# A decoder step with 16 experts on one core: order of the down weights, bf16 token tables, expert 0's table first, tail transposes between halves

## The chip, the cores and the metric

The kernel runs on one core of a Trainium2 chip. The metric is the time of one execution on the device in microseconds. The kernel before was timed three times: 1049.95 us median, 1045.94 to 1050.38.

## The reference

One layer of a decoder trunk serves 512 prompt tokens and 8 sample tokens (520 in all, width 1024). A joint projection feeds three attention-like heads (a gated recurrence, differential attention, dilated windows); their outputs are multiplied with `w_out` and added to the input. Then comes the part that the change touches:

```
u = rmsnorm(h) * norm_ffn
group = argmax(u @ rgw + rgb)                 # 4 groups
top 2 of the group's 4 experts, gate = p(group) * softmax(their logits)
for e in 16 experts:
    y += gates[:, e] * ((silu(u @ wg[e]) * (u @ wu[e])) @ wd[e])   # 1024 -> 512 -> 1024
h = h + y
h = h + sigmoid(rmsnorm(h) * norm_ple @ pgw) * (p @ ppw)
y_out = rmsnorm(h) * norm_final
```

All arrays are float32. An expert has three weights of 2 MB: gate and up (1024 x 512) and down (512 x 1024), 100 MB for the sixteen.

## The kernel before

There are five instruction streams, one per engine, and all order is by semaphores. Up to about 630 us the kernel computes the projection, the heads and `w_out` (L2262), and for each of five token tiles the normalised rows (stored to `u2d` in DRAM by SP, L750) and the router's logits.

**Routing.** VectorE turns the logits into one-hot choices, and `C` (128 tokens x 5 tiles x 16 experts) says which experts a token uses. TensorE multiplies `C` with a strict triangle `tri` and with `ones` (L2337 to L2341, float32, into PSUM bank 1): each token's rank within its expert and the count of each expert. VectorE sorts the experts by count (`key`, `beats`, `rnk`), plans the overflow, and gives every choice a row `rk` and a table column `tk` (L1804 to L1830). `Rsel` (L1831) and `Tsel` (L1832, L1833) are one-hot matrices of those, `Tsel` scaled by the token number, and ten float32 products (L2345) make of them a table of 33 columns with the token numbers of each expert job. VectorE computes the table of steps first and only then copies the token table to `idxall` (L1845). GpSimd copies one column of it (L862) and gathers the rows from `u2d` by an indirect DMA (L865), one gather for each step. The ranks of experts 0, 1 and 2 are fixed, so they are always the first three steps.

**Expert steps.** 15 static steps and a loop (one turn here) for the overflow follow. Step s handles 32 x `STEP_JOBS[s]` token rows: 3 jobs in steps 0, 1, 2, 6, 8, 10, 12, 14, 4 jobs in step 4, 2 jobs in the others. The first two jobs are one phase, what is left a second phase. In a phase:
- `rows` (L2354) transposes the gathered rows, VectorE's `front` (L1865) scales them to `xgT`;
- `gate_up` (L2369, and L2365 in the second phase of a 3-job step) multiplies 32 rows at a time with gate and up, four 32-column blocks of the array side by side. In the second phase of a 3-job step the four blocks hold the halves of gate and up, and a half is columns j, j+1 of every four: the moving operand is read with a step of four floats;
- ScalarE applies silu, VectorE multiplies, `columns_of_h` (L2389) transposes, ScalarE copies, `down` (L2406, and L2402 in such a second phase) multiplies with the down weights, VectorE copies the result, ScalarE's queue stores it to `Yd`.

TensorE runs a phase's `gate_up` before the `down` of the phase before.

**Weights.** `SLOT` has eight places of 2 MB, used in turn by the three loads of each step. SP issues the loads in order (L732); load k of step s waits until the `gate_up` or `down` that used its slot has ended (`released`). Loads of steps 1 and 0 and two of step 2 are issued before the routing, at 572 and at 630 us; the others wait. Each load moves 128 runs of 16 KB. After the loop's loads SP issues `ple_w_gate` (L775), `ple_w_proj` (L777), the p rows (L780) and `norm_final` (L781). The queues of SP, ScalarE and GpSimd use the same 16 DMA engines.

**Tail.** From 950 us TensorE transposes the p rows (L2320) and multiplies them (L2331), and then for each of five tiles: GpSimd gathers the two expert results, VectorE combines them (L1903, L1905), ScalarE computes the norm (L1143 to L1146), VectorE scales (L1913), TensorE transposes (`columns`, L2238), VectorE copies to `hnT` (L1920), TensorE multiplies with `ple_w_gate` in two halves of 16 records (`ple`, L2485; L2248 for the sample tile), ScalarE applies the sigmoid (L1239, L1242), VectorE finishes (L1662, L1663) and applies the last norm (L1669). `columns(i + 1)` stands behind both halves of `ple(i)`.

## Time and profile before

| | us |
|---|---|
| median of three runs | 1049.95 |
| the profiled execution | 1055.73 |
| its span | 1054.0, mean granted clock 0.948 |
| TensorE busy in it | 948.5 (90%) |
| VectorE, ScalarE, GpSimd busy | 376.9, 238.2, 81.5 |
| routing, from the last logits to the first expert product | 631.4 to 663.5 |
| expert steps | 663.5 to 950.1 |
| products of the p rows, then the tiles | 950.2 to 1051.6 |

Some single instructions that the text uses: VectorE had been idle for 2.67 us before its first `w_out` addition (L1707) at 564.35; `rows` of step 0 took 1.53 us from 660.91 and `front` 0.97 from 662.47; the operations between 642.28 (L1812) and 649.40 (L1832) end with the positions of all choices; of the products of the p rows the first eight records took 5.40 us from 954.36, the next eight 3.44; tile 1's scaling (L1913) ended at 981.77; the steps 8 and 9 began at 808.51 and the next at 842.34; SP issued the load of `ple_w_gate` at 922.95.

The profile is of one execution. Busy times of TensorE are of modelled ends: a float32 product shows as two records. The chain of waits follows the end of the program back from releaser to releaser; "landing" of a DMA is the time from its issue to its completion.

### The profile page before, as it was taken

Reading aid. Unit: us, or ns where it says so; the run is one execution under the profiler, and the core shown is the slowest. Engines: PE = TensorE matmul, PEld = TensorE weight load, DVE = VectorE, ACT = ScalarE, POOL = GpSimd, SP = SyncE. Lnnn points to the kernel's source line nnn. Section 1 sums busy time; section 2 is a strip of 40 time slices with the busy share of each in tenths; the row PEclk is TensorE's granted clock in tenths of the full one; section 3 lists DMA queues with packets and bytes.
Section 4 is the critical chain, followed back from the end, with each engine's and each line's share of the span. In section 5 each row is a group of like instructions: output and inputs, shape, how many; then the busy total and the mean of one; then the engine's idle time right before and its main releaser. Section 6 shows DMA issues by size and latency. Waiting matters only on the chain.

```text
span 1054.0 us, 15610 instructions
## 1 busy us (share of the span) xinstructions
PE 948.5 (90%) x6377; PEld 492.1 (47%) x6377; DVE 376.9 (36%) x791; ACT 238.2 (23%) x600; POOL 81.5 (8%) x96
## 2 busy tenths in 40 slices
PE   3996999999999998986969983899999999998886
PEld 2453556655456785663444543333333333333442
DVE  4305644564226755355542226111111111111445
ACT  3115212221232332443221110000000000003335
POOL 1000000000024531000000000100000000002100
PEclk9999999999999998969788995899999999999998
DMA  6463433035357651247323419298999999994101
GB/s 209 167 233 150 91 140 140 1 140 175 140 177 244 218 171 43 98 138 208 124 79 130 187 51 390 79 344 332 378 373 381 398 395 392 401 379 132 41 21 62
DMA packets 69138, 209.55 MB, mean 199 GB/s; under 512 B 19113, under 2 KB 51332, under 8 KB 62540
## 3 DMA queue, kind: packets, MB, share of 16 engines
q1 hardware_dynamic: 54384, 185.53, 47.8%
q0 software_dynamic: 3936, 14.22, 4.1%
q10 hardware_dynamic: 10748, 8.80, 2.6%
q8 instruction: 51, 0.84, 0.3%
q14 instruction: 19, 0.16, 0.0%
HBM read 189.09 MB, written 38.26 MB: 216 GB/s over the span
## 4 chain that ended last, share of the span: by engine, by line
PE 80%; DVE 8%; DMA 4%; ACT 4%; issue 2%; SPq 2%; ACTq 0%; POOL 0%; DVEq 0%; POOLq 0%
PE ps L1959 16%; PE ps L2369 11%; PE ps L1964 9%; PE ps L2262 6%; PE ps L2406 5%; PE ps L2485 5%; PE ps L2365 5%; DMA EXPERT<-in_moe_w_up 2%; PE ps L1994 2%; PE ps L2331 2%; PE ps L2040 2%; PE ps L2354 1%; PE ps L1968 1%; PE ps L2402 1%; PE ps L2121 1%
## 5 line engine op out<-in xcount | busy, mean ns | idle before, releaser
L1959 PE MATMUL ps<-xT,EXPERT 128*128 128x512 f32 x384 | 178.3, 610 | 1.2 <-DVE xS L1299 1.2
L1964 PE MATMUL ps<-EXPERT,xT 128*128 128x384 f32 (+1 forms) x384 | 121.6, 459 | 1.6 <-ACT EXPERT L959 1.6
L1959 PEld LDWEIGHTS ps<-xT,EXPERT 128*128 128x128 f32 x384 | 71.1, 195 | 77.3 <-issue 73.9
L1964 PEld LDWEIGHTS ps<-EXPERT,xT 128*128 128x128 f32 x384 | 78.7, 239 | 24.5 <-issue 3.6
L1871 DVE TENSOR_TENSOR dF<-dF,ps 64x512 f32<-64x512 f32 (+1 forms) x24 | 14.4, 601 | 185.3 <-ACT dF L1191 185.3
L2485 PE MATMUL ps<-EXPERT 128*128 128x512 f32 x128 | 56.0, 596 | 5.3 <-DVE EXPERT L1920 5.3
L2262 PE MATMUL ps<-EXPERT,xT 128*128 128x512 f32 x128 | 59.5, 617 | 0.8 <-ACT xT L1127 0.8
L2369 PE MATMUL ps<-EXPERT,samp 128*32 128x512 f32 x384 | 57.8, 594 | 0.0
L2369 PE MATMUL ps<-EXPERT,wk 128*32 128x512 f32 x448 | 53.2, 619 | 2.1 <-DMA EXPERT<-in_moe_w_up 1.1
L1195 ACT ACTIVATE dF<-ps 128x256 f32<-128x256 f32 (+1 forms) x24 | 8.3, 348 | 163.7 <-PE ps L2389 163.7
L1023 ACT ACTIVATE wk<-ps,small 128x128 f32<-128x128 f32 (+3 forms) x48 | 24.9, 522 | 85.5 <-DVE small L1460 85.5
L2406 PE MATMUL ps<-EXPERT,dF 128*32 128x512 f32 x384 | 43.8, 594 | 0.0
L1460 DVE TENSOR_REDUCE small<-ps 128x2 f32<-128x256 f32 (+3 forms) x24 | 19.8, 823 | 67.0 <-PE ps L2043 67.0
L2485 PEld LDWEIGHTS ps<-EXPERT 128*128 128x128 f32 x128 | 24.0, 190 | 34.9 <-issue 28.7
L2365 PE MATMUL ps<-EXPERT,wk 128*32 128x256 f32 x320 | 38.1, 630 | 0.0
L2262 PEld LDWEIGHTS ps<-EXPERT,xT 128*128 128x128 f32 x128 | 24.5, 198 | 28.5 <-issue 28.4
L842 POOL TENSOR_TENSOR aF<-aF 128x1536 f32<-128x1536 f32 x4 | 13.7, 3432 | 295.0 <-DMA aF<-q_d 295.0
L959 ACT ACTIVATE EXPERT<-ps 128x384 f32<-128x384 f32 (+2 forms) x36 | 17.6, 490 | 76.8 <-PE ps L1964 39.3
L1191 ACT ACTIVATE dF<-ps 64x512 f32<-64x512 f32 (+1 forms) x24 | 12.5, 519 | 90.6 <-PE ps L2369 63.5
L1420 DVE COPY_PREDICATED wk<-lmask,ps 128x384 f32<-128x384 uint8 x56 | 29.4, 579 | 9.9 <-PE ps L1994 9.6
L862 POOL COPY samp<-samp 128x1 int32<-128x1 int32 (+1 forms) x17 | 3.1, 183 | 361.8 <-PE ps L2354 244.8
L1881 DVE COPY wk<-ps 128x512 f32<-128x512 f32 (+1 forms) x24 | 14.5, 603 | 45.5 <-PE ps L2406 40.8
(457 smaller groups left out, 1353.2 us busy)
## 6 DMA issues: line engine op xcount, KB each, us to landing
EXPERT<-in_moe_w_gate SPq DMA_DIRECT2D x12, 2048.0 KB, 19.4
EXPERT<-in_moe_w_up SPq DMA_DIRECT2D x12, 2048.0 KB, 14.8
EXPERT<-in_moe_w_down SPq DMA_DIRECT2D x12, 2048.0 KB, 17.2
EXPERT<-in_w_in SPq DMA_DIRECT2D x13, 1536.0 KB, 6.6
out_win_sample<-in_cache_win SPq DMA_DIRECT2D x16, 1022.0 KB
aF<-in_cache_k_diff SPq DMA_DIRECT2D x32, 192.0 KB, 2.5
aF<-in_cache_v_diff SPq DMA_DIRECT2D x32, 192.0 KB, 2.5
Yd<-wk ACTq DMA_DIRECT2D x34, 128.0 KB, 8.5
```

What stands on the lines that cost most here:

```text
L1023: last = s.activation(wk[:, n % 2, m * SEQ:m * SEQ + K], ps[:, 2 + 2 * (n % 2) + m, 0:K], ACT.Exp, bias=negm[:, 2 * (n % 2) + m:2 * (n % 2 ...
L1420: last = v.copy_predicated(att, lmask[:, l - 1].unsqueeze(1).to_broadcast([P, 3, P]), src)
L1959: last = t.matmul(ps[:, u % 2, :], W_[:, c, c0:c0 + w], xT[:, c, 0:SEQ], start=(c == 0), stop=(c == DC - 1))
L1964: last = t.matmul(ps[:, u % 2, 0:w], rows_, W_[:, c, c0:c0 + w], start=(c == 0), stop=(c == DC - 1))
L1994: last = t.matmul(ps[:, 2 + 2 * (k % 2) + e, c * P:(c + 1) * P], L[h, c, :], R[h, c, :], start=True, stop=True)
L2040: t.matmul(ps[:, 2 + 2 * (n % 2) + m, 0:K], dF[r, 0, c, i * P:(i + 1) * P], dF[r, 1, c, 0:K], start=True, stop=False)
L2262: last = t.matmul(ps[:, 2 + 2 * (p % 2) + hf, :], xT[:, c, i * P:(i + 1) * P], wout_[c][:, hf * 512:(hf + 1) * 512], start=(c == 0), stop= ...
L2331: last = t.matmul(ps[0:r, 4 + 2 * (i % 2) + hf, :], pTt[i % 2][:, c, 0:r], plp_[:, c, hf * 512:(hf + 1) * 512], start=(c == 0), stop=(c == ...
L2365: last = t.matmul(ps[32 * q:32 * q + 32, bank, 0:256].rearrange("p (j a) -> p j a", j=2), x[:, c, 64:96], w.rearrange("p (a j) -> p j a", ...
L2369: last = t.matmul(ps[32 * q:32 * q + 32, bank, :], x[:, c, at:at + 32], w, start=(c == 0), stop=(c == DC - 1))
L2406: last = t.matmul(ps[32 * q:32 * q + 32, 5 + k, :], hidT[k][:, at:at + 32], w[:, hf * 512:(hf + 1) * 512], start=(f == 0), stop=(f == FC - 1))
L2485: last = t.matmul(ps[0:r, 4 + 2 * (i % 2) + hf, :], hnT[i % 2][:, c, 0:r], ple_[:, c, hf * 512:(hf + 1) * 512], start=(c == 0), stop=(c == ...
```

## The change

- The down weights are loaded with `s=2`: partition p gets rows 2p, 2p+1 of each half of the matrix, two runs of 8 KB. `columns_of_h` transposes hidden columns in the same order, and in second phases of 3-job steps `gate_up` reads 256 contiguous columns.
- `tri`, the ones, `C`, `Rsel` and `Tsel` become bf16. A token number is split into its low seven bits and the rest (`parts`), so there are two products for each of the ten one-hot matrices. The rank products move to PSUM bank 6.
- Expert 0's table is made first: `pos0` and `R0` right after the ranks, ten one-column products to bank 2, `idx0`, and its gather from `idx0` without a column copy. The products of the full table come after `rows(0)` on TensorE; on VectorE `front` of step 0 comes before the copy to `idxall` and before the table of steps.
- In the tail `columns(i + 1)` stands between the two halves of `ple(i)`. VectorE combines tile i + 1 right after the copy of tile i, and does the last norm of tile i - 2 before `finish(i - 1)`; ScalarE computes the norm of tile i + 1 before the sigmoid of tile i - 1.

```diff
-                    a["moe_w_down"][0].rearrange("e (p c) n -> p e (c n)", p=P)]
+                    a["moe_w_down"][0].rearrange("e (s p c) n -> p e s (c n)", s=2, p=P)]
...
+            g.indirect_dma_start(out=xg[0][0:32 * STEP_JOBS[0]], out_offset=None, in_=u2d,
+                                 in_offset=bass.IndirectOffsetOnAxis(ap=idx0[0:32 * STEP_JOBS[0]], axis=0)).then_inc(xgload[0], 16)
+            pool.wait_ge(S_["list_ok"], 2)
...
+            seq(v.tensor_copy(iti[:, 0:T5], tokf))
+            seq(v.tensor_scalar(iti[:, T5:2 * T5], iti[:, 0:T5], P - 1, None, ALU.bitwise_and))
+            seq(v.tensor_tensor(iti[:, 0:T5], iti[:, 0:T5], iti[:, T5:2 * T5], ALU.subtract))
+            for k in range(2):
+                v.tensor_copy(parts[:, k * T5:(k + 1) * T5, 0], iti[:, T5:2 * T5])
+                seq(v.tensor_copy(parts[:, k * T5:(k + 1) * T5, 1], iti[:, 0:T5]))
...
+            v.tensor_copy(partsb, parts[:, 0:T5])
+            seq(v.tensor_scalar(early, iotaf, 32.0 - 1024.0, None, ALU.add))
+            seq(v.tensor_scalar(early[:, 64:96], iotaf[:, 64:96], -64.0 - 1024.0, None, ALU.add))
...
+            seq(v.scalar_tensor_tensor(out=pos0, in0=C[:, :, 0], scalar=-1024.0, in1=ranks[:, :, 0], op0=ALU.mult, op1=ALU.add))
+            v.tensor_tensor(R0, early.unsqueeze(1).to_broadcast([P, T5, P]), f2(pos0, P), ALU.is_equal).then_inc(S_["rank_ok"], 1)
             seq(v.scalar_tensor_tensor(out=key, in0=cnt, scalar=float(NE), in1=krev, op0=ALU.mult, op1=ALU.add))
...
+            dve.wait_ge(S_["list_pe"], 1)
+            v.tensor_copy(idx0, ps[:, 2, 0:1]).then_inc(S_["list_ok"], 1)
             seq(v.tensor_tensor(n8, f2(over, 8), kcon.unsqueeze(1).to_broadcast([P, NE, 8]), ALU.is_gt))
...
+            seq(v.tensor_tensor(hot, iotaf[:, 0:MAXT].unsqueeze(1).to_broadcast([P, 2 * T5, MAXT]), f2(tk, MAXT), ALU.is_equal))
+            v.tensor_tensor(Tsel, hot.unsqueeze(2).to_broadcast([P, 2 * T5, 2, MAXT]), f3(parts, MAXT),
+                            ALU.mult).then_inc(S_["rank_ok"], 1)
+
+            front(1, 0, 32 * STEP_JOBS[0])
+            dve.wait_ge(S_["list_pe"], 2)
+            v.tensor_copy(idxall, ps[:, 6, 96:96 + MAXT]).then_inc(S_["list_ok"], 1)
             seq(v.tensor_tensor(xcmp, incl.unsqueeze(1).to_broadcast([P, NE + 1, NE]), f2(xrow, NE), ALU.is_le))
...
             pe.wait_ge(S_["rank_ok"], 1)
+            for i in range(T5):
+                for k in range(2):
+                    last = t.matmul(ps[:, 2, 0:1], R0[:, i], partsb[:, i, k:k + 1], start=(i + k == 0), stop=(i + k == T5))
             last.then_inc(S_["list_pe"], 1)
...
-                            j = 2 * (q % 2)
-                            last = t.matmul(ps[32 * q:32 * q + 32, bank, 0:256].rearrange("p (j a) -> p j a", j=2), x[:, c, 64:96],
-                                            w.rearrange("p (a j) -> p j a", j=FC)[:, j:j + 2], start=(c == 0), stop=(c == DC - 1))
+                            last = t.matmul(ps[32 * q:32 * q + 32, bank, 0:256], x[:, c, 64:96],
+                                            w[:, 256 * (q % 2):256 * (q % 2) + 256], start=(c == 0), stop=(c == DC - 1))
...
-            pe.wait_ge(S_["list_ok"], 1)
             rows(0, 32 * STEP_JOBS[0], 16)
+            pe.wait_ge(S_["rank_ok"], 2)
+            for m in range(2 * T5):
+                for k in range(2):
+                    last = t.matmul(ps[:, 6, 96:96 + MAXT], Rsel[:, m], Tsel[:, m, k], start=(m + k == 0),
+                                    stop=(m + k == 2 * T5))
+            last.then_inc(S_["list_pe"], 1)
...
                 for hf in range(2):
+                    if hf:
+                        columns(i + 1)
                     for c in range(DC):
```

## Rows read from the trace of the kernel before

**Rows 1.** The page's 40 slices of the span, busy tenths of the DMA engines.
```profile
DMA  6463433035357651247323419298999999994101
```

**Rows 2.** Windows: length, busy us by engine, granted clock, DMA share, GB/s.
```profile
745.00:945.00 200.00, 198.88 (x1838) 72.08 (x1826) 30.86 (x47) 15.54 (x35) 11.18 (x20) 1.00 1.01 393
...
681.00:745.00 64.00, 64.00 (x618) 23.92 (x618) 10.52 (x16) 4.88 (x12) 4.53 (x8) 1.00 0.88 321
...
640.00:655.00 15.00, 4.83 (x22) 4.59 (x22) 11.67 (x40) 0.00 (x0) 0.00 (x0) 0.50 1.00 429
```

**Rows 3.** Chain of waits (start, us, what), and the page's groups.
```profile
887.30 23.63 DMA EXPERT<-in_moe_w_up
...
L2369 PE MATMUL ps<-EXPERT,wk 128*32 128x512 f32 x448 | 53.2, 619 | 2.1 <-DMA EXPERT<-in_moe_w_up 1.1
```

**Rows 4.** Timeline of the SP queue (start, us): expert loads, norm_final last.
```profile
681.17 0.33 SPq L732 DMA_DIRECT2D EXPERT<-in_moe_w_down  x1
...
694.79 0.34 SPq L732 DMA_DIRECT2D EXPERT<-in_moe_w_up  x1
...
702.77 0.33 SPq L732 DMA_DIRECT2D EXPERT<-in_moe_w_down  x1
...
716.40 0.33 SPq L732 DMA_DIRECT2D EXPERT<-in_moe_w_up  x1
...
724.38 0.33 SPq L732 DMA_DIRECT2D xT<-in_moe_w_down  x1
...
739.19 0.33 SPq L732 DMA_DIRECT2D EXPERT<-in_moe_w_up  x1
...
937.07 1.06 SPq L781 DMA_DIRECT2D EXPERT<-in_norm_final  x1
```

**Rows 5.** DMA issues; landings of the loads at 694.79, 739.19, and 13 gathers.
```profile
EXPERT<-in_w_in SPq DMA_DIRECT2D x13, 1536.0 KB, 6.6
...
EXPERT<-in_ple_w_gate SPq DMA_DIRECT2D x1, 4096.0 KB, 21.1
...
EXPERT<-in_norm_final SPq DMA_DIRECT2D x1, 512.0 KB, 12.7
...
DMA to landing us min/median/max: 8.0/8.0/8.0
...
DMA to landing us min/median/max: 10.5/10.5/10.5
...
DMA to landing us min/median/max: 5.5/10.2/11.7
```

**Rows 6.** Chain of waits, 630 to 665 us: routing and first gather.
```profile
635.91 0.71 PE ps L2337 x2
...
640.39 0.19 DVE samp L1804
...
648.00 1.49 DVE dF L1831
...
656.91 3.86 DMA PT<-u2d,samp
```

**Rows 7.** Timeline of TensorE at 663.48; chain of waits, 680 to 700.
```profile
663.48 9.62 PE L2369 MATMUL ps<-EXPERT,wk 128*32 128x512 f32 x64 [1.05 <-DVE wk L1865]
...
693.00 1.73 PE ps L2402 x32
...
694.73 3.62 PE ps L2365 x32
```

**Rows 8.** Timeline of TensorE at 950.18; chain of waits in the tail.
```profile
950.18 0.66 PE L2320 MATMUL ps<-ident,EXPERT 128*128 128x128 f32 x4
...
991.69 1.24 DVE EXPERT L1920
...
992.97 14.00 PE ps L2485 x32
...
1039.36 0.60 PE ps L2238 x8
```

More of the change, by code:

```diff
@@ L485, in hybrid_kernel @@
         toki = take(T5, dt=I32)
-        tri = take(P)
+        tri = take(P // 2, dt=BF16)
+        onesb = take(P // 2, dt=BF16)
+        parts = take(2 * T5, 2)
+        partsb = take(T5, dt=BF16).rearrange("p (i a) -> p i a", i=T5)
+        early = take(P)
+        pos0 = take(T5)
+        idx0 = take(1, dt=I32)
         before = take(4, 4)
@@ L497, in hybrid_kernel @@
         O12, t12 = take(2 * T5, NE), take(2 * T5, NE)
-        C = take(T5, NE)
+        C = take(T5 * NE // 2, dt=BF16).rearrange("p (i e) -> p i e", i=T5)
         gm, gs, gw, e2, w1, w2 = (take(T5) for _ in range(6))
@@ L504, in hybrid_kernel @@
         nx, incl, exc = (take(NE) for _ in range(3))
-        Tsel = take(2 * T5, MAXT)
+        hot = take(T5 * MAXT, dt=BF16).rearrange("p (m j) -> p m j", m=2 * T5)
+        Tsel = take(2 * T5 * MAXT, dt=BF16).rearrange("p (m a j) -> p m a j", m=2 * T5, a=2)
         xcmp = take(NE + 1, NE)
@@ L866, in gather @@
                                      in_offset=bass.IndirectOffsetOnAxis(ap=idxc[b][0:r], axis=0)).then_inc(xgload[b], 16)
-            for step in range(NE):
+            for step in range(1, NE):
                 if step >= 2:
@@ L871, in _ @@
                 r = RANK_AT[step]
-                gather(slice(r, r + 1), step % 2, 32 * JOBS[r], step + 1)
+                gather(slice(r, r + 1), step % 2, 32 * JOBS[r], step)
             pool.wait_ge(S_["tab_rdy"], 1)
@@ L876, in _ @@
                 pool.wait_ge(S_["mx_pe"], i + NE)
-                gather(bass.ds(i + NE, 1), 1, 64, i + NE + 1)
+                gather(bass.ds(i + NE, 1), 1, 64, i + NE)
             pool.wait_ge(ystore[0], STORED[0])
@@ L1250, in _, with tile_rms @@
                 pcolumns(i + 2)
-            for i in range(T5):
+            def tile_rms(i):
                 act.wait_ge(S_["comb_ok"], i + 1)
                 inv_rms(i, "hn_e")
-                if i == 0:
-                    pproducts(T5 - 2)
-                    pproducts(T5 - 1)
+            tile_rms(0)
+            pproducts(T5 - 2)
+            pproducts(T5 - 1)
+            tile_rms(1)
+            for i in range(1, T5):
                 if i >= 2:
@@ L1259, in _ @@
                     inv_rms(i - 2, "n4_e")
-                if i:
-                    gate(i - 1)
-                    s.preload_act_table_set("natural_log_exp_and_others")
+                if i < NT:
+                    tile_rms(i + 1)
+                gate(i - 1)
+                s.preload_act_table_set("natural_log_exp_and_others")
             gate(NT)
@@ L1677, in _, with front @@
                     does[step](*arg)
+            def front(n, b, r):
+                dve.wait_ge(S_["mx_pe"], n)
+                v.tensor_tensor(xgT[b][:, :, 0:r], ps[:, 0:2, :].rearrange("p b (c t) -> p (b c) t", c=4)[:, :, 0:r],
+                                f2(gruns[:], r), ALU.mult).then_inc(S_["mx_ok"], 1)
             dve.wait_ge(S_["iot"], 1)
@@ L1898, in _, with combine @@
                 v.tensor_copy(yb_[1][:, 0:512], ps[:, 5, :]).then_inc(S_["yc_ok"], 1)
-            for i in range(T5):
+            def combine(i):
                 r = tile_rows(i)
@@ L2491, in _ @@
                 ple(i)
-                if i < NT:
-                    columns(i + 1)
 INS = ['x_prompt', 'x_sample', 'state_hgrn', 'cache_k_diff', 'cache_v_diff', 'cache_win128', 'cache_win512',
```

49 lines of the change are left out of this document (24 added, 25 removed).

## The prediction

> **What bounds the kernel now.** I read the page's busy shares and slices first: TensorE is busy 90% of the span, and in slices 29 to 36 of 40 the DMA row stands at 9 beside it [rows 1]. So an average does not say which of the two sets the pace of the expert stage, and I went to the windows. From 745 to 945 us TensorE is busy 198.9 of 200 us at full clock and the DMA engines have work all the time (share 1.01) at 393 GB/s; from 681 to 745 the DMA share is 0.88 [rows 2]. The chain of waits then names the one place where the DMA decides: the up weights of expert step 14, issued at 887.30, landed 23.63 us later at 910.9, and TensorE had waited only 1.1 us for them [rows 3]. A load alone on the queues lands in 8.0 us (issued 694.79), the one issued at 739.19 in 10.5, and at 887.30 the lag is 23.6 [rows 3 to 5]. The lag grows through the stage, and the DMA is slightly slower than TensorE: 27 loads of 2 MB land between 749.7 (739.19 + 10.5) and 910.9, 5.97 us each, stores and gathers between them included, or 35.8 us for two steps. TensorE needs 33.9 for two (808.5 to 842.3, steps 8 and 9). It is a tie that DMA is about to win, and whatever makes TensorE faster there is given back in waits.
>
> Outside it, two stretches are TensorE and VectorE alone. From 631.4 to 663.5 the routing runs through small VectorE operations, short products at half clock and one gather [rows 6], while ten MB of weights stream in at 429 GB/s [rows 2]. From 974 the last stage goes tile by tile with a gap between tiles [rows 8].
>
> **Part 1, the half phases.** Eight of the fifteen static steps have three jobs, and each has a second phase whose gate/up products read the weights with a step of four floats (L2365), 32 records in 3.62 to 3.74 us, twice per phase. That is what 32 records of twice the width take (L2369: 3.43 to 3.57), while the down products of the same width but contiguous (L2402) take 1.73 to 1.86 [rows 7]. The change reads contiguously, so each half phase should drop from 7.4 to 3.6, by 3.76 us, eight times 30 us. Below: if the stride is not the reason, nothing goes; above: no more than the L2402 rows.
> Beside it, by the Trainium skill (SBUF — State Buffer, the note on 16-byte cachelines), reads that jump to a new line each time pay for it; the rows agree, and by it the 30 us hold.
>
> How much of 30 survives is set by the loads. The slots are released by these very phases: SP's issues follow the end of step 0's gate/up (681.2, two loads, the second a us later), its down (694.8, one), then step 1 (702.8, two; 716.4, one) and step 2 (724.4, two; 739.2, one) [rows 4]. I let each load take 5.97 us of the queue from its release or from the load before, and land 3 us later (8.0 alone, less some 5 of transfer). Before: the ninth leaves at 745.2 and lands at 748.2 (trace: 749.7). After, the releases come 3.76, 3.76, 7.5, 7.5, 11.3 and 11.3 us earlier (677.4, 691.0, 695.3, 708.9, 713.1, 727.9); the queue is busy to 689.3, 697.0, 708.9, 714.9, 726.8, 733.9, and the ninth lands at 736.9. That is 11.3 us, and from there the queue never empties, so every later landing moves by 11.3. Bounds: 3.8 (only the first release counts) and 15.6 (all 11.8 us between 68.5, the measured time of the nine, and 9 × 5.97 + 3, come back). The rest of the 30 us turns into waits of TensorE for the up weights: step 10 about 3 us, steps 12 and 14 about 6 each.
>
> **Part 2, the 8 KB runs.** Same bytes, twice the packets for 14 loads still to come. The 1.5 KB rows of in_w_in move 1.57 MB in 6.6 us, the 16 KB runs 2.1 MB in 8.0 [rows 5]: less the 3 us, 437 and 420 GB/s. I take zero. Against it: ple_w_gate (4 KB rows, backlogged) lands 21.1 us after 922.95, some 13 us after the load before it, where two expert loads take 10 to 12; at that rate each down load costs up to 1.3 us, 18 in all.
>
> **Part 3, the early start.** Rank products: 20 float passes take 635.91 to 640.39 at half clock, 0.224 each [rows 6]; in bf16 one pass each of 10, between 0.11 (half the time) and 0.224: 1.1 to 2.2, I take 1.5, so 637.4. VectorE then adds pos0 (0.2) and R0 (640 elements, half of L1831's 1.49: 0.77) to 638.4; ten one-column products (1.1 to 2.2, take 1.3) run beside the seven operations that stood between 640.39 and 642.28 (1.9), to 640.3; copy idx0 0.2; GpSimd needs no index copy and starts the gather at 641.0 instead of 656.91 [rows 6]. But it no longer finds free queues: before it landed in 3.9 us after the loads had drained, while the 13 gathers inside the saturated stretch took 5.5 to 11.7, median 10.2 [rows 5]. So 651.2. Transposes 1.53, then 20 bf16 list products (2.2 to 4.5, take 2.3) queue on TensorE ahead of gate/up, hiding front (0.97): gate/up starts at 655.1 instead of 663.48, 8.4 us earlier. VectorE has the tables at 640.5 + 7.1 (642.28 to 649.40) + 0.45 + 0.77 = 648.9, before they are wanted; front is now behind them, and idxall, the table of steps and tab_rdy behind front, some 659.5. The next gather (then issued near 657) and tab_rdy are both needed near 669, when step 0's gate/up ends. Bounds: 12.3 (gather in 3.9, held by the tables at 648.9) and 4.8 (11.7, and 4.5 for the products). The ten constant operations added at 561.7 take 0.17 to 0.22 each like the ten beside them, 2.0, inside VectorE's 2.7 us of idle before L1707 (in the table of the profile): zero, and at most 0.5 without that cover.
> Beside it, the Trainium skill (DMA: Bandwidth & Descriptors, "Queues, rings and completion order") says a DMA engine takes turns between queue rows by packets. By it the gather overtakes the queued loads, as the 10.2 does; by strict order it would land near 659, which is a rival below. No run here shows a gather amid these five loads.
>
> **Part 4, the tail.** Between tiles TensorE transposes (0.89), VectorE copies (1.24), and the next products start 2.19 us after the last [rows 8]. With the transposes between the halves, 0.89 stays and 1.30 goes, three times, and 0.44 before the sample tile (1.04 less 0.60): 4.3. The columns must be ready at each middle: tile 1's rows are scaled by 981.8, the middle is 983.8; later ones come some 8 us ahead. At the end ScalarE needs gate(3) and two table loads, 3.6 us from 1039.39, and the sample product now gives it 3.7 instead of 4.7: just enough. I take 4.2; bounds 3.0 (every middle waits a little) and 5.5.
>
> **The sum.** The load of step 14 lands at 910.9 − 8.4 − 11.3 = 891.2. TensorE needed 39.1 us from there to 950.18 (first transposes of the last stage) [rows 8], now 35.4: ready at 926.6. What it then waits for are the ple rows: the last load behind them, issued 937.07, lands 12.7 us later at 949.8, they about 1.2 sooner, 948.6 [rows 4, 5]; less 8.4 and 11.3, 19.7, that is 928.9. So the late thing moves from TensorE to the DMA, and the stage starts 21.3 us earlier. With the tail: 25.5. The profiled execution took 1055.73 (span 1054.0, 1.7 around it) and would take 1030.2; it lay 5.8 above the median, and against that median, 1049.95, I say 1024.5.
>
> **Rivals.**
> (a) The gather waits until the loads have drained: lands near 659, gate/up starts 663, early start worth 0.5. Gain 17.6: 1032.5. For it the 16 KB packets ahead of it; against it the 10.2 us amid backlogs of 20. Chance 0.14.
> (b) TensorE's clock. From 640 to 655, nearly idle, it had 0.50, and step 0's first 64 records, after that, took 9.62 instead of 7.0 [rows 2, 7]. If each new wait of 3 to 6 us does that, step 14 ends 2.6 later (929.2, level with the ple rows), and the ple products, eight records of which took 5.40 instead of 3.44, lose up to 2 more: 1028. Chance 0.12. Beside it, the Trainium skill (TensorE: Matmul & The Clock Gate, Part 1) says the throttled state is the default and idleness brings it back; by it this rival holds at all three waits. Before, 1.1 us of wait at 911 left the clock at 1.00.
> (c) TensorE alone sets the pace, the DMA finds more rate: 8.4 + 30 + 4.3, 42.7: 1007. The 429 GB/s of 640 to 655 speak for it, the share of 1.01 against. Chance 0.06.
> (d) The stride is not the reason, L2365 stays at 3.6: 8.4 + 4.2: 1037. The L2402 rows speak against. Chance 0.05.
> (e) Slower: down loads in 8 KB runs are slow. The queue is the bound, so each us counts for 14 loads; from 25.5 / 14 = 1.8 us per load on the change loses. Were they to take twice 5.2 us, 73 more: 1097. The in_w_in rows speak against. Chance 0.04.
> My forecast has 0.59.
>
> **Range and chances.** The unknowns at their lower ends, 4.8 + 3.8 + 3.0, give 1038; at their upper, 12.3 + 15.6 + 1.6 + 5.5, give 1015. With (a), (b) and (d) inside and (c), (e) out: 1013 to 1038. About 0.5% is what a measurement can tell. Only (e) is not faster, and a little of it ends within: faster 0.94, same 0.02, slower 0.04.
>
> **What would show it.** Right: L2365 at 1.8 us for 32 records; gate/up of step 0 starting near 655; DMA share 1.0 from about 670 until the ple rows; new waits of TensorE on the up weights before steps 10, 12, 14; no gap of 2.2 in the tail. Wrong: a down load that lands later than an up load in the same place; no new waits (c); a gather landing at 659 (a); DMA share under 0.95 with TensorE waiting.

## The result, and the profile after

The changed kernel takes 1015.64 us (median of 4 runs, 1011.32 to 1018.23) beside 1050.16 (1045.94 to 1054.6) of the kernel before: a ratio of 0.9673, 95% interval 0.964 to 0.9706, or 34.5 us. Forecast were 1024.5 us, within 1013 to 1038. A second set of five runs, beside the experiments, gave 1018.73 us and 0.9688 (0.9659 to 0.9718). One execution each of e1 (2309 us), e9 (1538) and the kernel before (1152) was slow far beyond all others and is left out of the medians and ratios below.

The profiled execution of the changed kernel has a span of 1015.0 us, against 1054.0. Not all of these 39.0 us belong to the change. The last routing logits come out of code that the change leaves alone; here is the line that computes them in the kernel before, the changed kernel, and the changed kernel profiled a second time (columns: durations in ns, start of the first and of the last in us).

```profile
L1739 DVE SCALAR_TENSOR_TENSOR samp<-ps,small,rbias x5: 220/238/239, 589.0 to 631.4; 128x20 f32<-128x20 f32 x4, 8x20 f32<-8x20 f32 x1
```

```profile
L1772 DVE SCALAR_TENSOR_TENSOR samp<-ps,small,rbias x5: 220/238/239, 579.8 to 623.0; 128x20 f32<-128x20 f32 x4, 8x20 f32<-8x20 f32 x1
```

```profile
L1772 DVE SCALAR_TENSOR_TENSOR samp<-ps,small,rbias x5: 220/239/240, 585.1 to 627.5; 128x20 f32<-128x20 f32 x4, 8x20 f32<-8x20 f32 x1
```

631.4, 623.0 and 627.5: one and the same kernel differs from itself by 4.5 us there, and over all fourteen profiled executions of this study the mark lies between 623.0 and 634.1. The traces part where the granted clock dips in different places: between 540 and 560 us it is 0.69 in the kernel before, 0.94 in the changed one and 0.78 in its second profile. So I measure every profile from its own last logits. The table has, for all kernels, the median and ratio of their runs, and from the profile the last logits, then the way from there to the first gate/up product, from that to the last gate/up product, to the first product of the p rows, and to the end; the last column is the sum of these four. The expectations of the runs quote such sums 600 us too high (992 is 392.0, 983.5 is 383.5); their differences are right. e4, e5 and e6 put out other values than the reference: they serve for their times alone.

| kernel | median, us | ratio, 95% | logits at | to gate/up | gate/up | to p rows | to end | sum |
|---|---|---|---|---|---|---|---|---|
| before | 1050.16 | 1 | 631.4 | 32.1 | 279.8 | 11.1 | 99.6 | 422.6 |
| changed | 1015.64 | 0.9673 (0.964–0.9706) | 623.0 | 21.5 | 265.0 | 11.0 | 94.5 | 392.0 |
| changed, again | 1018.73 | 0.9688 (0.9659–0.9718) | 627.5 | 21.5 | 264.7 | 12.7 | 94.5 | 393.4 |
| e1 layout alone | 1035.68 | 0.9851 (0.9819–0.9883) | 623.9 | 32.1 | 263.0 | 12.8 | 100.5 | 408.4 |
| e2 tables alone | 1039.11 | 0.9871 (0.9837–0.9905) | 632.4 | 23.5 | 278.0 | 11.0 | 97.9 | 410.4 |
| e3 tail alone | 1043.68 | 0.9918 (0.9888–0.9947) | 626.3 | 32.2 | 278.4 | 11.0 | 95.5 | 417.1 |
| e4 16 KB runs | 1021.00 | 0.9719 (0.9677–0.9761) | 625.9 | 23.4 | 261.7 | 11.0 | 94.5 | 390.6 |
| e5 stride back | 1036.66 | 0.9863 (0.9816–0.991) | 624.7 | 21.4 | 278.1 | 12.7 | 94.5 | 406.7 |
| e6 fewer bytes | 1005.07 | 0.9548 (0.9506–0.959) | 632.0 | 21.3 | 248.0 | 12.7 | 94.5 | 376.5 |
| e7 late gather | 1032.12 | 0.9813 (0.977–0.9855) | 625.6 | 35.0 | 262.8 | 12.7 | 95.5 | 406.0 |
| e8 p rows first | 1019.33 | 0.9689 (0.9639–0.9738) | 633.8 | 21.6 | 261.1 | 11.5 | 92.8 | 387.0 |
| e9 clear gather | 1012.20 | 0.9646 (0.9603–0.969) | 634.1 | 17.7 | 265.2 | 11.5 | 92.8 | 387.2 |
| e10 full filler | 1021.56 | 0.9725 (0.9697–0.9754) | 623.5 | 21.5 | 265.0 | 11.4 | 94.5 | 392.4 |
| e12 half the filler | 1013.38 | 0.9631 (0.9581–0.9682) | 627.5 | 17.7 | 263.8 | 9.7 | 92.8 | 384.0 |

The change is worth 30.6 us by that sum (29.2 against its second profile): 10.6 in the routing, 14.8 in the gate/up stretch, 5.1 in the tail.

Two columns carry a step that has nothing to do with the edits. Of "to p rows", the last 32 down products took 3.64 us in some kernels and 5.1 to 5.3 in others, with no wait for data ahead of them: in the changed kernel 3.64 (granted clock 1.00, column 11.0), in its second profile 5.34 (clock 0.66, column 12.7). Of "to end", the first eight records of the p rows took 3.70, 5.40 or 6.3 us: 5.40 in the kernel before and both profiles of the changed one, 3.70 in e2, e8, e9 and e12, 6.3 in e1, e3 and e7.

The page's DMA slices of the changed kernel, which answer to [rows 1]: 9 from slice 27 on, not 29.

```profile
DMA  6444631232447753153623705799999999996111
```

The windows, as in [rows 2]. The share of 0.88 that stood after step 0 is 0.99 now, and it is TensorE that falls short, with 90.4 busy us of the last 100.

```profile
655.00:670.00 15.00, 15.00 (x158) 6.16 (x158) 2.07 (x3) 1.32 (x4) 1.11 (x2) 1.00 0.77 269
670.00:740.00 70.00, 70.00 (x730) 28.11 (x723) 11.90 (x18) 6.47 (x15) 4.51 (x8) 1.00 0.99 385
740.00:800.00 60.00, 60.00 (x616) 23.46 (x619) 10.78 (x16) 4.63 (x12) 4.46 (x8) 1.00 1.01 386
800.00:900.00 100.00, 90.41 (x885) 36.07 (x881) 15.09 (x23) 7.81 (x18) 5.57 (x10) 0.93 0.99 393
```

What TensorE waited for between 640 and 960 us (total, times, longest). Before, the loads had cost it 1.1 us here [rows 3]; now 9.6 in three waits.

```profile
PE ps L2398 <- DMA PT<-u2d,samp: 11.9, 1, 11.9
PE ps L2412 <- DMA EXPERT<-in_moe_w_up: 5.7, 2, 3.7
PE ps L2412 <- DMA aF<-in_moe_w_up: 3.9, 1, 3.9
PE ps L2363 <- DMA EXPERT<-in_p_sample: 2.3, 1, 2.3
PE ps L2535 <- DVE EXPERT L1957: 1.3, 1, 1.3
PE ps L2374 <- ACT EXPERT L1185: 1.2, 1, 1.2
```

TensorE's timeline through the routing, one wait of the stage, its end, and the tail (start, length, what, idle before it). L2380 to L2389 and L2467 are bf16 now; 844.02 is step 12, whose first 32 records take 6.45 us (3.64 for the next 32, at 851.01); from 949.93 the transposes of the next tile lie between two halves.

```profile
627.53 0.25 PE L2380 MATMUL ps<-samp 128*128 128x80 bf16 x1 [4.53 <-DVE samp L1818]
627.58 0.34 PE L2382 MATMUL ps<-samp 128*128 128x64 bf16 x4
627.77 0.28 PE L2384 MATMUL ps<-samp 128*128 128x16 bf16 x5
629.55 0.43 PE L2389 MATMUL ps<-samp,dF 128*128 128x1 bf16 x10 [1.50 <-DVE dF L1838]
641.87 1.54 PE L2398 MATMUL ps<-ident,PT 96*128 96x96 f32 x8 [11.89 <-DMA PT<-u2d,samp]
643.21 0.78 PE L2467 MATMUL ps<-samp,dF 128*128 128x33 bf16 x20
...
844.02 6.45 PE L2412 MATMUL ps<-EXPERT,wk 128*32 128x512 f32 x32 [3.74 <-DMA EXPERT<-in_moe_w_up]
...
851.01 3.64 PE L2412 MATMUL ps<-EXPERT,wk 128*32 128x512 f32 x32
...
879.18 5.34 PE L2412 MATMUL ps<-EXPERT,wk 128*32 128x512 f32 x32 [1.98 <-DMA EXPERT<-in_moe_w_up]
884.45 0.69 PE L2432 MATMUL ps<-ident,dF 64*128 64x64 f32 x4
...
918.73 0.66 PE L2363 MATMUL ps<-ident,EXPERT 128*128 128x128 f32 x4 [2.30 <-DMA EXPERT<-in_p_sample]
920.53 5.40 PE L2374 MATMUL ps<-EXPERT 128*128 128x512 f32 x8 [1.15 <-ACT EXPERT L1185]
...
949.93 1.04 PE L2281 MATMUL ps<-ident,wk 128*128 128x128 f32 x8
950.80 13.90 PE L2535 MATMUL ps<-EXPERT 128*128 128x512 f32 x32
```

The half phases: this is the gate/up line of old L2365 [rows 7] (ns minimum, median, maximum).

```profile
L2408 PE MATMUL ps<-EXPERT,wk x320: 379/379/403, 653.3 to 896.0; 128*32 128x256 f32 x160
```

### The profile page after: what moved, and what is told of

Its sections match the earlier page's. It is cut to its first block, busy times and chain, and to the rows that moved or that the text cites. A ratio compares the mean times of both kernels' runs of the same rounds, so it can differ in the third digit from the quotient of the medians.

```text
span 1015.0 us, 15620 instructions
## 1 busy us (share of the span) xinstructions
PE 914.1 (90%) x6377; PEld 484.7 (48%) x6377; DVE 381.2 (38%) x804; ACT 238.6 (24%) x600; POOL 82.0 (8%) x96
## 4 chain that ended last, share of the span: by engine, by line
PE 76%; DMA 9%; DVE 7%; ACT 4%; issue 2%; SPq 2%; ACTq 0%; DVEq 0%; POOLq 0%
PE ps L2002 17%; PE ps L2412 11%; PE ps L2007 9%; PE ps L2305 6%; PE ps L2535 5%; PE ps L2449 5%; DMA EXPERT<-in_moe_w_up 4%; DMA aF<-in_moe_w_up 2%; PE ps L2037 2%; PE ps L2374 2%; PE ps L2408 2%; PE ps L2083 2%; PE ps L2011 1%; PE ps L2110 1%; PE ps L2398 1%
## 5 line engine op out<-in xcount | busy, mean ns | idle before, releaser
L2412 PE MATMUL ps<-EXPERT,wk 128*32 128x512 f32 x448 | 57.1, 657 | 6.2 <-DMA EXPERT<-in_moe_w_up 5.7
L2305 PE MATMUL ps<-EXPERT,xT 128*128 128x512 f32 x128 | 57.2, 597 | 1.1 <-ACT xT L1142 1.1
L2305 PEld LDWEIGHTS ps<-EXPERT,xT 128*128 128x128 f32 x128 | 23.5, 190 | 27.2 <-issue 27.1
L2412 PEld LDWEIGHTS ps<-EXPERT,wk 128*32 128x32 f32 x448 | 15.1, 119 | 39.3 <-issue 38.2
L1158 ACT ACTIVATE PT<-XM 128x1024 f32<-128x1024 f32 (+1 forms) x15 | 15.8, 1055 | 59.4 <-DVE XM L1938 23.8
L2037 PEld LDWEIGHTS ps<-wk 64*128 64x128 f32 x336 | 20.9, 187 | 18.5 <-DVE wk L1425 9.2
```

Source lines behind the costliest of these rows:

```text
L2037: last = t.matmul(ps[:, 2 + 2 * (k % 2) + e, c * P:(c + 1) * P], L[h, c, :], R[h, c, :], start=True, stop=True)
L2305: last = t.matmul(ps[:, 2 + 2 * (p % 2) + hf, :], xT[:, c, i * P:(i + 1) * P], wout_[c][:, hf * 512:(hf + 1) * 512], start=(c == 0), stop= ...
L2412: last = t.matmul(ps[32 * q:32 * q + 32, bank, :], x[:, c, at:at + 32], w, start=(c == 0), stop=(c == DC - 1))
```

## The experiments

**Each part alone: e1, e2, e3.** Three kernels, the one before with one part of the change each. They also split the result.

e1 has the new arrangement of the down weights and the reads that it allows:

```diff
-                sp.dma_start(SLOT[slot(step, kind)].unsqueeze(1),
+                sp.dma_start(SLOT[slot(step, kind)].rearrange("p (e s n) -> p e s n", e=1, s=(1, 1, 2)[kind]),
...
-                            last = t.matmul(ps[32 * q:32 * q + 32, bank, 0:256].rearrange("p (j a) -> p j a", j=2), x[:, c, 64:96],
+                            last = t.matmul(ps[32 * q:32 * q + 32, bank, 0:256], x[:, c, 64:96],
```

> The kernel before with the down weights' new arrangement and the half phases that read neighbouring columns, and nothing else of the change. My theory: the half phases fall from 7.4 to 3.6 us, the loads then set the pace, and the stretch from the first gate/up product to the landing of step 14's up weights shrinks as in the changed kernel (247.5 to 234.6 us, 12.9 us): 1037 us, between 1034 and 1041. Rival 'TensorE alone': all eight half phases count, 30 us, 1020 us. Rival 'the stride is not what slows them': half phases stay at 7.4 us and the time at 1050 us. Rival 'the 8 KB runs cost': slower than 1050 us.

1035.68 us. The gate/up stretch goes from 279.8 to 263.0. Of these 16.8 us the last down products, at the lower clock here (5.34 us for 3.64), take 1.7 back, and the first eight records of the p rows 0.9; from the last logits 14.2 us are gone, 15.7 by the ratio. The loads' limit is in its trace too: TensorE waits 10.4 us in three times.

e2 has the bf16 tables and expert 0's own table and gather (all of the change's edits but those of e1 and e3).

> The kernel before with the bf16 token tables and expert 0's own table and gather ahead of the sorting of the others, and nothing else. My theory: the stretch from the last logits to the first gate/up product goes from 32.1 to 21.4 us, and since TensorE sets the pace afterwards here, the 10.6 us stay whole to the end: 1040 us, between 1038 and 1043. Rival 'the start is paid back': the loads cannot run ahead by as much, TensorE waits for them later, and less than half of it is left: 1045 us or more. Under both the first gate/up product is 21 to 22 us after the last logits.

1039.11 us. The start comes 8.6 us sooner, not 10.6, since this gather took 11.6 us to land (issued 641.75, its rows on TensorE at 653.31) where the changed kernel's took 9.5. It all stays: 12.2 us by the sum, 13.6 by the ratio; the 3.6 us beyond the start lie in stretches whose instructions are those of before: 1.7 are the first eight records of the p rows (3.70 us for 5.40), 1.8 the gate/up stretch, and I count both to the scatter.

e3 has the order of the tail alone:

```diff
+                for hf in range(2):
+                    if hf:
+                        columns(i + 1)
```

> The kernel before with the new order of the last stage alone (transposes between the halves). My theory: 4 to 5 us from the stretch after the first p product (99.6 to 94.5 us in the changed kernel): 1045.5 us, between 1044 and 1047. Rival 'cover gone': ScalarE's gates, which come out just in time in the changed kernel, come late, and 2 us or less is left: 1048 us or more.

1043.68 us, 0.3 below its bounds; 8.6 by the ratio, 5.5 by the sum. The tail goes from 99.6 to 95.5, by 4.1, although the first eight records of the p rows took 6.32 us for 5.40; without that it is 5.0, as in the changed kernel (5.1). ScalarE's gates come in time. By the sum the three parts give 14.2 + 12.2 + 5.5 = 31.9 us, against 30.6 together; by the ratios 37.9 against 34.5. Within that scatter they add up.

**Do the 8 KB runs cost? e4.**

```diff
-                sp.dma_start(SLOT[slot(step, kind)].rearrange("p (e s n) -> p e s n", e=1, s=(1, 1, 2)[kind]),
+                sp.dma_start(SLOT[slot(step, kind)].rearrange("p (e s n) -> p e s n", e=1, s=1),
```

> The changed kernel with the down weights read in 16 KB runs as before (one run of memory per partition; the rows then meet the wrong rows of the activations, so the output of the experts is another one), everything else as changed. My theory: the length of the run costs nothing, the landings of down loads stay as they are (median 18.0 us) and so do the 5.9 us per load: 1015.6 us, within 3 us. Rival 'the 8 KB runs cost': each of the down loads comes faster, and with the loads setting the pace 16 of them give back 0.3 us or more each: 1010 us or less.

1021.0 us, no faster than either set of the changed kernel (0.9719 against 0.9673 and 0.9688, intervals that overlap). The gate/up stretch of its profile is 261.7, 3 us shorter than the changed kernel's, but kernels with 8 KB runs and the same loads show 261.1 and 262.8 too (e8, e7). Rival (e) falls; a price below 0.2 us per load can't be told from the scatter.

**Is it the stride? e5.**

```diff
-                            last = t.matmul(ps[32 * q:32 * q + 32, bank, 0:256], x[:, c, 64:96],
-                                            w[:, 256 * (q % 2):256 * (q % 2) + 256], start=(c == 0), stop=(c == DC - 1))
+                            j = 2 * (q % 2)
+                            last = t.matmul(ps[32 * q:32 * q + 32, bank, 0:256].rearrange("p (j a) -> p j a", j=2), x[:, c, 64:96],
+                                            w.rearrange("p (a j) -> p j a", j=FC)[:, j:j + 2], start=(c == 0), stop=(c == DC - 1))
```

> The changed kernel, with the gate and up products of the half phases reading every fourth column as before instead of 256 neighbours (the columns of step halves then come out in another order, so the experts' output is another one); the load, the down products and all else stay as changed. My theory: the 32 products of each such quarter go from 1.86 back to 3.7 us or so, and the stretch of the gate/up products grows from 265.0 by at most the 16.8 us that the layout took off it: 1028 us, between 1024 and 1033. Rival 'the stride is not what slows them' (the gain came from the new landings or the down products alone): 1016 us, within 3 us. Rival 'the strided gate/up products account for all 30 us': 1037 us or more.

The same line in e5, same tiles, same shape:

```profile
L2409 PE MATMUL ps<-EXPERT,wk x320: 610/632/637, 654.0 to 910.4; 128*32 128x256 f32 x160
```

A record lasts 632 ns instead of 379: the stride is the reason. The stretch is 278.1, 13.1 more, and TensorE no longer waits for a single load. The time, 1036.66, is outside my range of 1024 to 1033 and 0.3 us short of where the second rival began: by the ratio 18 to 20 us above the changed kernel, by the sum 13 to 15. The times alone don't exclude that rival; the profile does, since the stretch that holds the edit grew by 13.1 and not by 30. What the rest is I can't say.

**Who paces the stage? e6.**

```diff
             def load(step, kind, e):
+                if kind == 2 and step >= FIXED:
+                    sp.dma_start(SLOT[slot(step, kind)].rearrange("p (e s n) -> p e s n", e=1, s=2)[:, :, 0:1],
+                                 wsrc[kind][:, bass.ds(e, 1), 0:1]).then_inc(wload[slot(step, kind)], 16)
+                    return
```

> The changed kernel, with only one half of the down weights loaded from step 3 on (the other half of each tile keeps what it held; the output is another one): 13 of the 39 loads are half as long, so five sixths of the bytes. My theory: the loads set the pace of the changed kernel, so TensorE's three landings' waits (9.6 us together) and the slow products behind them (17.1 us for three times 32 products instead of 10.3) go and TensorE alone paces the stretch: 265.0 us becomes 249, the time 1000 us, between 995 and 1005. Rival 'the waits are not the loads' pace but their late release': most of them stay, 1011 us or more.

1005.07 us, just above the range, and the stretch is 248.0 for an expected 249. Its waits in the same range as above:

```profile
PE ps L2402 <- DMA PT<-u2d,samp: 11.7, 1, 11.7
PE ps L2378 <- ACT EXPERT L1189: 3.5, 1, 3.5
PE ps L2539 <- DVE EXPERT L1961: 1.3, 1, 1.3
```

No wait for a load is left, and the DMA share falls to 0.94 at TensorE's full 160 of 160 us:

```profile
740.00:900.00 160.00, 160.00 (x1658) 63.95 (x1654) 27.69 (x42) 13.41 (x31) 10.08 (x18) 1.00 0.94 359
```

So 248.0 us is what TensorE needs, and the other kernels can be added up from it. In the changed one, the 32 records behind each wait hold TensorE for 5.26, 6.38 and 5.27 us until the next instruction (808.21 to 813.47, 844.02 to 850.40, 879.18 to 884.45), where e10 below shows 3.55 at full clock: 6.3 us lost. 248.0 + 9.6 of waits + 6.3 = 263.9, for 265.0 measured. Its second profile waited in the same three places, for 4.8, 1.1 and 6.1 us, and lost 4.4: 264.4, for 264.7. The same sum for e1, e4, e7, e8 and e9 comes out 0.4 to 1.4 us below their stretches. In e5, 248.0 + 8 × 3.76 of stride = 278.1, for 278.1. So the layout did take all 30 us off TensorE, and the loads let 13 of them through. Behind the vanished wait for the p rows stands one of 3.5 us for ScalarE's first copy, which I had not seen, though the kernel before has it at the same place:

```profile
954.36 5.40 PE L2331 MATMUL ps<-EXPERT 128*128 128x512 f32 x8 [3.52 <-ACT EXPERT L1170]
```

**Does a later start carry through? e7.**

```diff
+            pool.wait_ge(wload[slot(2, 1)], 16 * uses(2, 1))
             g.indirect_dma_start(out=xg[0][0:32 * STEP_JOBS[0]], out_offset=None, in_=u2d,
```

> The changed kernel, with GpSimd holding expert 0's gather until the up weights of step 2 have landed (653.7 instead of 632.3 us in the profiled execution); nothing of the computation changes. My theory: the gather then lands within 4 to 5 us, the first gate/up product starts some 16 us later, at 37 us after the last logits instead of 21.5, and as the next loads are released by those products the whole of it is carried to the end: 1031 us, between 1027 and 1034. Rival 'the loads have slack': TensorE catches up with the loads, half or less is left at the end: 1024 us or less.

1032.12 us. GpSimd issues the gather at 653.77 on empty queues, and TensorE has its rows at 658.02, 4.3 us later. By the sum the first gate/up product is 13.5 us later than in the changed kernel, the end 14.0 (12.6 against its second profile); by the ratios 13 to 15. So a later start is carried to the end, and a rival (a) that held the gather back by as much would have cost that.

**The p rows: e8.**

```diff
-            sp.dma_start(ple_[:, :, :], a["ple_w_gate"][0].rearrange("(c p) n -> p c n", p=P)).then_inc(S_["pleload"], 16)
             sp.wait_ge(gu_pe[0], phases_in(0, STATIC))
...
+            sp.dma_start(ple_[:, :, :], a["ple_w_gate"][0].rearrange("(c p) n -> p c n", p=P)).then_inc(S_["pleload"], 16)
             sp.dma_start(nfin, a["norm_final"].rearrange("(o n) -> o n", o=1).to_broadcast([P, D])).then_inc(S_["pleload"], 16)
...
-            s.preload_act_table_set("natural_log_exp_and_others")
             pcolumns(0)
             pcolumns(1)
+            s.preload_act_table_set("natural_log_exp_and_others")
```

> The changed kernel, with the load of ple_w_gate issued behind the per-layer-embedding rows instead of ahead of them, and ScalarE's table load behind the first two row transposes' copies. Nothing of the computation changes. My theory: TensorE's wait of 2.3 us for the last of these rows goes, and of the 1.15 us for the first copy most: 1012.5 us, between 1011 and 1014. Rival 'ple_w_gate is late instead': the first gate product of the last stage waits for its landing (22 us after its issue in the changed kernel, which would be 930 us, before it is needed at 943): the same as the changed kernel, 1015 us or more.

1019.33 us, no difference from the changed kernel that can be measured, and outside the 1011 to 1014 that I gave. The wait for the rows is gone and TensorE never waits for `ple_w_gate`; what is left of the gain stands behind what e6 had shown. ScalarE's timeline of e8 at the place:

```profile
926.15 1.17 ACTq L1244 DMA_DIRECT2D Yd<-wk  x2
927.52 0.66 ACT L1185 ACTIVATE EXPERT<-ps 128x256 f32<-128x256 f32 x2 [7.83 <-issue]
928.19 1.28 ACT L1262 ACT_TABLE_LOAD   x1
```

The first copy stands behind the issue of the last two stores, and TensorE waits 2.24 us for it, where the second profile of the changed kernel had waited 0.54 + 2.91. That profile is the one to compare with, since its last down products took 5.34 us, as e8's did: from the last gate/up to the first p product 12.7 became 11.5, 1.2 us instead of 3.3. The 1.7 us behind it are the first eight records (3.70 us for 5.40); e2 has them as short behind an unchanged wait of 3.51 us, so they can't be put down to the edit. I had read the last releaser of a wait as the whole of it.

**The changed kernel once more.**

> The changed kernel once more, beside the next two on the same chip. Expected under every theory: 0.967 of the kernel before, some 1016 us, and 992 us from the last logits to the end, give or take 4 us; the time of the last logits itself anywhere between 623 and 634 us, as in the ten profiled executions so far.

0.9688 and 393.4 us, logits at 627.5: as expected.

**A gather on clear queues: e9** (with the edits of e8).

```diff
-            for kind in range(3):
+            for kind in range(2):
                 load(0, kind, 0)
-            load(2, 0, 2)
             sp.wait_ge(S_["rl_pe"], T5)
+            sp.wait_ge(xgload[0], 16)
+            load(0, 2, 0)
+            load(2, 0, 2)
             load(2, 1, 2)
```

> The changed kernel with the two edits of the run before (per-layer-embedding rows ahead of ple_w_gate, table load behind two copies), and with SP sending only the gate and up weights of expert 0 before expert 0's gather; its down weights and step 2's gate and up weights wait until the gather has landed. Nothing of the computation changes. My theory: the gather takes 9.5 us in the changed kernel because it shares the DMA engines with five loads; with two, gone after some 11 us, it takes 4 to 5 us, the first gate/up product starts 3 to 4 us sooner (18 us after the last logits instead of 21.5, then bound by the tables), and all of it is kept: 1011 us, between 1008 and 1014, and some 983.5 us from the last logits to the end. Rival 'the held loads are missed': the idle DMA engines between the two groups put step 2's gate and up weights and all that follows later, and TensorE waits longer for loads afterwards: 1015 us or more.

TensorE's wait for the gather, in its trace:

```profile
PE ps L2400 <- DMA PT<-u2d,samp: 7.2, 1, 7.2
```

Issued at 643.37, with the two loads nearly through (DMA share 0.58 in the 4.8 us that it takes), the rows are there at 648.25: 4.9 us, not 9.5. The start is 17.7 us after the logits, as I said, and the gate/up stretch is 265.2, that of the changed kernel: nothing of the held loads is missed. By the sum e9 is 4.8 to 6.2 us ahead of the changed kernel's two profiles; its median of 1012.2 is within my range, but the ratio, 0.9646 (0.9603–0.969), overlaps that of the changed kernel, so the runs alone don't show it faster. The 383.5 that I expected had e8's stretch of 261.1 in it, which was a lucky one.

**TensorE busy in the waits: e10.**

```diff
+            def filler(step, bank, n):
+                x = xgT[step % 2]
+                for i in range(n):
+                    for q in range(4):
+                        t.matmul(ps[32 * q:32 * q + 32, bank, 0:256].rearrange("p (c t) -> p c t", c=4), x[:, i % DC, 0:32],
+                                 x[:, 4 * (i % 2):4 * (i % 2) + 4, 0:64], start=True, stop=True)
...
+                    if step in (10, 12, 14):
+                        filler(step, 2 + p % 2, {10: 14, 12: 14, 14: 10}[step])
```

> The changed kernel with TensorE kept busy in its three waits for the up weights of steps 10, 12 and 14: ahead of each it computes 56, 56 and 40 products of 32 by 256 of the rows at hand, which nothing reads (3.0, 3.0 and 2.1 us at full clock). My theory: the products behind the waits then run at full clock (3.43 us for 32 instead of 5.34 to 6.45), but the loads set the pace, so what they gain at steps 10 and 12 comes back as a longer wait at the next load, and only the last 1.9 us are kept: 1014 us, between 1012 and 1017. Rival 'the clock's fall is what the waits cost': all 6.8 us are kept: 1009 us or less. Rival 'the filler is longer than the waits', which vary from run to run: 1018 us or more.

TensorE's timeline of e10:

```profile
840.85 6.23 PE L2421 MATMUL ps<-wk 128*32 128x256 f32 x112
846.89 3.62 PE L2412 MATMUL ps<-EXPERT,wk 128*32 128x512 f32 x32
...
877.06 4.50 PE L2421 MATMUL ps<-wk 128*32 128x256 f32 x80
881.38 3.62 PE L2412 MATMUL ps<-EXPERT,wk 128*32 128x512 f32 x32
```

The fillers take 6.23 us, twice my estimate (I had taken a record of the trace for a product; there are two to each). They replace the waits, and the products behind them run at full clock, 3.55 us to the next instruction. But they hold TensorE for 6.0, 6.0 and 4.3 us, 16.4 in all, as long as waits and slow products together (15.9), and the stretch is 265.0. The third rival, then: 1021.56 us is no gain, and whether the fall of the clock is what the waits cost stays open.

**e12, half the filler, on the best of the others.** Against e9: VectorE makes the first two copies of the p rows, and the fillers are 7, 7 and 5 rounds.

```diff
-            pcolumns(0)
-            pcolumns(1)
...
+            for i in range(2):
+                dve.wait_ge(S_["pp_t"], i + 1)
+                v.tensor_copy(pTt[i][:, :, 0:P],
+                              ps[:, 2 + i, 0:2 * P].rearrange("p (c t) -> p c t", c=PC)).then_inc(S_["pp_c"], 1)
             combine(0)
```

> The run with the held loads once more, with two further edits. VectorE, idle then, makes the first two copies of the per-layer-embedding rows in place of ScalarE, which there was still issuing its last stores; and TensorE computes 28, 28 and 20 products that nothing reads ahead of the waits at steps 10, 12 and 14 (3.1, 3.1 and 2.2 us by the 6.23 us that 56 of them took), half as many as in the run with all of them. Expected under every theory: 17.7 us from the last logits to the first gate/up product, and 1 to 1.5 us less than 11.5 between the last gate/up product and the first product of the per-layer embeddings. The theories part on the stretch of the gate/up products, 265.2 us in the run with the held loads, 265.0 and 264.7 in the changed kernel's two. My theory: the loads pace it and it stays at 263 to 265 us, the time at 1011 us, between 1008 and 1015. Rival 'the clock's fall is what the waits cost': it shrinks by 5 us or more, to 260 us or less, and the time is 1006 us. Rival 'the fillers outlast the waits': 267 us or more.

TensorE's timeline of e12:

```profile
804.92 3.21 PE L2425 MATMUL ps<-wk 128*32 128x256 f32 x56
...
838.22 3.21 PE L2425 MATMUL ps<-wk 128*32 128x256 f32 x56
845.67 6.01 PE L2416 MATMUL ps<-EXPERT,wk 128*32 128x512 f32 x32 [4.25 <-DMA EXPERT<-in_moe_w_up]
...
878.24 2.34 PE L2425 MATMUL ps<-wk 128*32 128x256 f32 x40
880.40 3.62 PE L2416 MATMUL ps<-EXPERT,wk 128*32 128x512 f32 x32
...
918.65 3.70 PE L2378 MATMUL ps<-EXPERT 128*128 128x512 f32 x8 [0.65 <-DVE EXPERT L1962]
```

Step 10 now starts at full clock without a wait, and the time comes back at step 12: 3.21 us of filler and 4.25 of wait, where e9 had waited 4.78. In both kernels the products of step 12 start 200.5 us after the first gate/up product (845.67 less 645.2, and 852.28 less 651.8): the load decides, whatever TensorE saved before. The stretch is 263.8. Fillers (3.0, 3.0, 2.2), wait (4.3) and the 2.4 us lost behind it are 14.9, and 248.0 + 14.9 = 262.9. So at steps 10 and 12 the fall of the clock is not what the waits cost. Behind the last wait, step 14's, nothing hands it back: e9 lost 1.7 us there (5.22 for 3.55), e12 none, and its stretch is 1.4 us shorter, less than single profiles differ (261.1 in e8, with the same loads and no filler). VectorE's copies take 1.8 us off the way to the first p product (11.5 to 9.7), and the whole is 384.0 us from the logits, 8.0 and 9.4 less than the changed kernel's two profiles. 0.9631 (1013.38 us) is the lowest ratio of a kernel with the right output, but its interval (0.9581 to 0.9682) overlaps those of e9 and the changed kernel, so the runs alone don't prove the gain.

## Why the prediction was right

**Part 1** was forecast at 11.3 us, within 3.8 to 15.6, and is 12.9: the landing of step 14's up weights lies 234.6 us after the first gate/up product (879.0 less 644.5) where it was 247.5. The half phases fell as said (32 records from 3.6 to 3.8 us to 1.9), and 27 loads land at 5.94 us each, as before at 5.97: the queue was already the limit there, and only the hole ahead of it (share 0.88) could be taken. The waits came before steps 10, 12 and 14, as 3.9, 3.7 and 2.0 instead of 3, 6 and 6 (4.8, 1.1 and 6.1 in the second profile). With the 6.3 us that the products behind them lost at the lower clock, or 4.4 in the second profile, they make 15.9 and 16.4 us, for a forecast 15: time lost behind one wait is missing from the next. So the mechanism of rival (b) is there, and at steps 10 and 12 without its price, as e12 shows. Its price behind step 14 is real: 1.7 us in the first profile (5.27 for 3.55), 1.6 in the second.
The Trainium skill (SBUF — State Buffer, the note on 16-byte cachelines) has reads that enter a new line each time pay for it; e5 against the changed kernel agrees, with 632 and 379 ns.

**Part 2** was zero, and e4 finds nothing above the scatter.

**Part 3** was forecast at 8.4 and is 10.6: a term sized too small. I took the bf16 products by half and whole float passes: 1.5, 1.3 and 2.3 us. They took 0.5 (627.53 to 628.05), 0.43 and 0.78, less than my lower ends. Little of the first two reached the gather, since VectorE stands beside them: R0 and the seven operations behind it end at 631.27, the one-column products already at 629.98, and the gather is issued 9.3 us after the logits for a forecast 9.6. It landed after 9.5 us for the forecast 10.2, amid five loads. From there to the first gate/up product it is 2.6 us instead of 3.9: the list products are 1.5 shorter, and TensorE then waits 0.48 for `front`, which they no longer hide. That is 0.3 + 0.7 + 1.3 of the 2.2 (rounded). The gathers of e2 and e4 took 11.6 and 11.5, so the gather alone moves the start by 2 us from kernel to kernel; e7 and e9 give the price of the crowd, 9.5 against 4.3 and 4.9.
The Trainium skill (DMA: Bandwidth & Descriptors, "Queues, rings and completion order") lets an engine take turns between queue rows; the gather that landed at 641.8, 12 us ahead of the last of the loads issued before it, agrees, and rival (a) falls.

**Part 4** was forecast at 4.2 and is 5.1, because beside the gaps the products of three tiles ran a little faster (13.73 us each for 14.00).

**The end of the stage** came out right by luck. The p rows became the late thing, with a wait of 2.30 us for a forecast 2.3. But I let that wait delay everything behind it, and it delayed nothing: ScalarE, behind its last stores and a table load, is what the first p product waits for in both kernels. That product starts 7.75 us after the last down products began in the kernel before (954.36 less 946.61) and 7.74 in the changed one (920.53 less 912.79). What took its place is the clock: step 14's products lost 1.7 us, which I had left to rival (b). From the landing of step 14's up weights to the first p product 1.9 us went (43.4 to 41.5), where I had 1.6 by two errors that nearly cancel: 2.3 for a wait without a price, and nothing for the slow products.

**The sum** was 25.5, and the profiles say 30.6 and 29.2. The terms missed by 2.2 (routing), 1.6 (part 1), 0.3 (end of the stage) and 0.9 (tail), all to the same side, so the range held and the middle was 9 us too high. The runs say 34.5 and 32.1 (1050.86 less 1018.73). The 2 to 4 us between runs and profiles are not explained: they may lie ahead of the logits, in code that is the same, where single profiles scatter by more. The same holds for the 5.8 us by which the profiled execution of before lay above its median.

**The rivals.** (a) falls with the landing at 641.8; (b) is there in part, as told above; (c), TensorE alone, is what e6 shows once bytes are taken away; (d) falls with e5, (e) with e4.

## What to carry to other kernels

Where an engine and the loads are tied, ask for the stretch with the loads made light, as e6 does: it gives the one number (here 248.0 us) by which every other variant can be added up, and it tells that 17 of 30 us saved on TensorE come back as waits and slow products. Measure a change from the last mark of code that it leaves alone: here that mark wanders by 11 us, more than most single parts are worth. And before a wait is removed, look up when the second releaser came: at the p rows ScalarE's copy came 1 us behind the rows, and the trace of the kernel before had already shown it.

## What the runs showed of the hardware

- At a granted clock of 0.50 a bf16 product of one column took 0.043 us (10 in 0.43) and one of 33 columns 0.039 (20 in 0.78), where a float pass of 33 columns had taken 0.224 (20 records in 4.47, kernel before).
- A gather of 96 rows lands in 4.2 and 4.8 us on clear or nearly clear queues (e7, e9) and in 9.3 to 11.5 with five 2 MB loads ahead (e6, e2), the last of which lands 30.4 us after its issue (changed kernel). It passes them, at twice its price.
- Reading the moving operand in steps of four floats, a record of 256 columns lasts 632 ns, and 379 with neighbouring columns; one of 512 neighbouring columns lasts 592. At that step the width halved saves nothing.
- Behind a wait of TensorE the next 32 records held it for 4.8 to 6.5 us instead of 3.55 in some cases and not in others, and the length of the wait does not sort them: slow behind 2.0 us (changed kernel), 2.4 (e9), 2.8 (e8), 2.9 (e1) and 3.7 to 7.7; at full clock behind 0.4 to 1.3, but also behind 2.4 and 2.7 (e4), 3.0 (e1) and 3.1 (e7). The same fall came with no such wait, at the last down products of eight of the fourteen profiles (5.1 to 5.3 us for 3.64).
